# First norm's scale and shift terms as matrix-vector products between the dense products of the first three weight tiles

## Chip, cores and metric

One core of a Trainium2 chip runs the whole program. The metric is device time in microseconds (us); the kernel before takes 3083.03 us, the median of three runs (3082.98 to 3083.45).

## The reference, cut to what matters

Two layers work on 512 latent tokens and 256 context tokens of width 1024. Every sublayer starts with a modulated RMS norm, and the modulation comes from a conditioning vector (`c` for latent tokens, `c_ctx` for context tokens) through one large matrix with nine terms of 1024 per layer:

```
def modulate(h, g, shift, scale):
    return rmsnorm(h, g) * (1 + scale) + shift
def adaln_terms(s, w, b):
    return jnp.split(jax.nn.silu(s) @ w + b, N_MOD, -1)
def swiglu(x, w_up, w_down):
    gate, up = jnp.split(x @ w_up, 2, -1)
    return (jax.nn.silu(gate) * up) @ w_down
```

The first sublayer is a SwiGLU. Its up product can't be finished before term 0 (shift) and term 1 (scale) of layer 0 are known, each 1024 values for two vectors. These two terms are what the change is about.

## The kernel before, in words

Activations lie feature-major: `h` is 8 tiles (KD) of 128 features by 768 tokens. A list of items (`schedule`, L83) gives the order of work, and each engine's program walks that list. A dense product (`dense_step`, L1771) has one weight tile of up to 8 row blocks; for each block it issues six TensorE matmuls: high weights by high activations, high by low, low by high, each in two column pieces of 384 or 386. The split into high (`wh`) and low (`wl`) parts is made on the chip: ScalarE makes the high part (L988), GpSimd the low part (L883).

The norm is applied late: the activations that go in are `h * scale`, the factor 1/rms is applied to the product. The shift goes in as one more column for each of the two token kinds (`shift_high` L1037, `shift_low` L1321).

**The start item.** The first three weight tiles (FUSED = 3) are worked together, feature tile by feature tile: for k = 0..7 TensorE waits for the split activations of tile k (`late_lo`, `shift_lo`, L1826 and L1827) and then runs 18 matmuls, six for each of the three weight tiles. What stands before tile k:

- The scale term is a matrix-vector product on TensorE (`start_scale`, L1791): 8 products with a 128x128 weight block as stationary side and the 2 columns of `c_cols` as moving side. Each appears as two instructions in the trace. Blocks 0 and 1 run ahead of the dense work, block k+2 runs behind dense tile k. VectorE turns the result into the gain (`start_gains`, L1416).
- The shift term is made off TensorE from another layout of the weights (`ada_start`, 8 loads): VectorE multiplies and sums for the latent vector (`ada_chunk`, L1529), GpSimd multiplies for the context vector (`context_shift`, L892), ScalarE sums that (L1165), VectorE adds the bias (`start_shifts`, L1422). Both need the conditioning vectors spread over all partitions (`cb`), which TensorE makes with 16 products against the identity (L1817), copied by VectorE and ScalarE (L1559, L1163).
- ScalarE makes the high part of `h * scale` (`late_high`, L1054) and the square of `h` (L997), VectorE the low part (`late_low`, L1340), GpSimd sums the squares (`start_square`, L902).

After tile 7 the norm item (L1853) sums over the features, ScalarE takes the root (L1186), and from then on TensorE goes through dense products.

The loads are all asked by SyncE's queue, in this order: `scale_w` 0, `h` 0, three weight tiles, `ada_start` 0, and then `scale_w`, `h`, `ada_start` for k = 1..7 (L717 to L722), then constants.

Of the kernel before, what the change touches and what calls it, by code (L numbers as in the profile page):

```python
# [4 lines left out]

D = 1024
# [20 lines left out]
ADA_FIRST = KD  # L27
# [167 lines left out]
def build(nc, a, out, items):  # L195
# [8 lines left out]
    ada_order = ada_chunks(0, [0]) + [c for i in sorted(plan) for c in plan[i]]  # L204
    ada_no = {c: n for n, c in enumerate(ada_order)}
    term_no = {c[:2]: n for n, c in enumerate([c for c in ada_order[ADA_FIRST:] if c[2] == KD - 1])}
    on_dve = lambda n: n if n <= ADA_FIRST else 2 * n - ADA_FIRST
# [30 lines left out]
    with ExitStack() as ctx:  # L238
# [33 lines left out]
        def region(name):  # L272
# [9 lines left out]
        ada_start = [tb(f"ada_start{i}", [P, D]) for i in range(ADA_FIRST)]  # L282
# [45 lines left out]
        start_product, context_product = ada_w[2], ada_w[0:2]  # L328
# [27 lines left out]
        ident_loaded, const_loaded = sem("ident_loaded"), sem("const_loaded")  # L356
        c_rows_made, c_rows_copied, context_multiplied, context_summed = (
            sem("c_rows_made"), [sem(f"c_rows_copied{v}") for v in range(2)], sem("context_multiplied"), sem("context_summed"))
        c_cols_loaded, terms_loaded = sem("c_cols_loaded"), sem("terms_loaded")
        tile_loaded = [sem(f"tile_loaded{i}") for i in range(KD)]  # L360
# [4 lines left out]
        start_loaded = [sem(f"start_loaded{i}") for i in range(ADA_FIRST)]  # L365
# [46 lines left out]
        def released(x):  # L412
# [5 lines left out]
            if kind == "start":  # L418
                return [(start_gain, KD)]
# [71 lines left out]
        def c_rows(v):  # L491
            return psum[:, D * v:D * v + D]

# [13 lines left out]
        CONSTS = 16 * 5  # L507
# [190 lines left out]
        def _(sp):  # L698
# [13 lines left out]
            def load_start(k):  # L712

                sp.dma_start(scale_w[k][:, :], a["scale_w"][k]).then_inc(tile_loaded[k], 16)
                sp.dma_start(h[:, k, :], a["xT"][:, k, :]).then_inc(tile_loaded[k], 16)
# [7 lines left out]
            for dst, src in ((mean_w, "mean_w"), (ones_w, "ones_w"), (dn_w, "dn_w")):  # L723
# [45 lines left out]
            asked = [ADA_FIRST]  # L769
            last_even = max((slot_of[x] for x in proj_order), default=0)  # L770

            def load_ada(last):

                upto = ADA_FIRST + sum(len(plan[i]) for i in plan if i <= last)
                for n in range(asked[0], upto):
                    sp.wait_ge(ada_summed, on_dve(max(ADA_FIRST, n - ADA_BUFS + 1)))
# [3 lines left out]
            for x in items:  # L780
# [56 lines left out]
                if x[0] == "proj" and x[1] == 0:  # L837
                    k = proj_order.index(x) - 12
                    if k == 0:
                        sp.wait_ge(bias_made, 16 * 3 * ROWS * NA_HEADS)  # L840
                        sp.wait_ge(ada_summed, on_dve(ADA_FIRST + sum(len(c) for i, c in plan.items() if i < number[x])))
# [27 lines left out]
        def _(pool):  # L869
# [3 lines left out]
            done = [0]  # L873

            def split_up_to(n_slots):

                while done[0] < min(n_slots, len(slots)):
                    n = done[0]
                    _, k, w = slots[n]
                    if n:  # L880
                        pool.wait_ge(lo_split, n)
# [10 lines left out]
            def context_shift(k):  # L892

                pool.wait_ge(start_loaded[k], 16)
                if k == 0:
                    pool.wait_ge(c_rows_copied[1], 1)
                if k >= 2:
                    pool.wait_ge(context_summed, k - 1)
                nc.gpsimd.tensor_tensor(context_product[k % 2][:, :], ada_start[k][:, :], cb[:, 1, :], ALU.mult) \
                    .then_inc(context_multiplied, 1)  # L900

            def start_square(k):  # L902

                pool.wait_ge(squared, k + 1)
                if k == 0:
# [1266 lines left out]
```

## Time and profile before

| what | value |
|---|---|
| median of 3 runs | 3083.03 us |
| profiled execution, its own time | 3078.91 us |
| its span | 3077.1 us |
| mean granted TensorE clock | 0.991 of full |
| TensorE busy | 97% of the span |
| first dense matmul of the start item | 26.88 us |
| first dense matmul behind the first norm | 78.22 us |

The profiled execution is 4.1 us below the median of the runs; 1.8 us of its time lie outside the span. The last two lines bound the stage in which the change works: from there on the program before and after is the same.

### The profile page before, as it was taken

Reading aid. Unit: us, or ns where it says so; the run is one execution under the profiler, and the core shown is the slowest. Engines: PE = TensorE matmul, PEld = TensorE weight load, DVE = VectorE, ACT = ScalarE, POOL = GpSimd, SP = SyncE. Lnnn points to the kernel's source line nnn. Section 1 sums busy time; section 2 is a strip of 40 time slices with the busy share of each in tenths; the row PEclk is TensorE's granted clock in tenths of the full one; section 3 lists DMA queues with packets and bytes.
Section 4 is the critical chain, followed back from the end, with each engine's and each line's share of the span. In section 5 each row is a group of like instructions: output and inputs, shape, how many; then the busy total and the mean of one; then the engine's idle time right before and its main releaser. Section 6 shows DMA issues by size and latency. Waiting matters only on the chain.

```text
span 3077.1 us, 45850 instructions
## 1 busy us (share of the span) xinstructions
PE 2971.3 (97%) x19023; PEld 2783.6 (90%) x19023; DVE 1601.0 (52%) x2437; ACT 985.4 (32%) x1701; POOL 996.5 (32%) x516
## 2 busy tenths in 40 slices
PE   6999999999989988999999999999999999999998
PEld 6999999999888875899999999999999877798997
DVE  6556666884646666477677684212122358431223
ACT  4211212343454457322121233212122347532222
POOL 5333333333332202233333333222222222344442
PEclk8999999999999999999999999999999999999999
DMA  4434454223320022234344342121211210232222
GB/s 190 137 113 132 128 140 141 87 87 118 116 68 15 8 80 77 76 130 137 130 130 145 109 131 66 61 66 60 65 62 55 74 49 2 63 102 91 90 95 70
DMA packets 126236, 284.25 MB, mean 92 GB/s; under 512 B 40222, under 2 KB 57550, under 8 KB 126030
## 3 DMA queue, kind: packets, MB, share of 16 engines
q1 hardware_dynamic: 123150, 274.86, 28.0%
q10 hardware_dynamic: 2880, 6.47, 0.5%
q8 instruction: 151, 2.47, 0.3%
q14 instruction: 55, 0.45, 0.0%
HBM read 269.68 MB, written 15.10 MB: 93 GB/s over the span
## 4 chain that ended last, share of the span: by engine, by line
PE 88%; DVE 5%; ACT 4%; issue 2%; POOL 0%; DMA 0%; ACTq 0%; SPq 0%; DVEq 0%; POOLq 0%
PE psum L1777 78%; PE psum L1952 2%; PE psum L2052 1%; DVE o_acc L1604 1%; PE psum L2040 1%; ACT prob_o L1258 1%; DVE prob_o L1708 1%; PE psum L1937 1%; PE psum L2033 1%; PE psum L1993 1%; PE psum L1972 1%; PE psum L1959 1%; ACT cacc L1112 0%; PE psum L1982 0%; DVE probT_o L1720 0%
## 5 line engine op out<-in xcount | busy, mean ns | idle before, releaser
L883 POOL TENSOR_TENSOR wl<-raw,wh 128x1024 fp32r<-128x1024 f32 (+1 forms) x329 | 837.8, 2547 | 1649.3 <-ACT wh L988 1648.0
L1777 PE MATMUL psum<-uh,wh 128*128 128x256 f32 (+5 forms) x2704 | 660.5, 325 | 27.7 <-DVE ul L1325 17.6
L1777 PE MATMUL psum<-ul,wh 128*128 128x256 f32 (+5 forms) x2704 | 659.0, 325 | 0.0
L1777 PE MATMUL psum<-uh,wl 128*128 128x256 f32 (+5 forms) x2704 | 658.8, 325 | 0.0
L1777 PE MATMUL psum<-ah,wh 128*128 128x386 f32 (+4 forms) x2192 | 595.4, 344 | 4.7 <-POOL wl L883 3.5
L1777 PE MATMUL psum<-ah,wl 128*128 128x386 f32 (+4 forms) x2192 | 590.6, 342 | 0.0
L1777 PE MATMUL psum<-al,wh 128*128 128x386 f32 (+4 forms) x2192 | 588.3, 341 | 0.0
L1777 PEld LDWEIGHTS psum<-uh,wh 128*128 128x128 f32 (+1 forms) x2704 | 451.1, 189 | 51.7 <-issue 24.7
L1529 DVE SCALAR_TENSOR_TENSOR ada_product<-ada_w,cb 128x1024 f32<-128x1024 f32 x256 | 478.2, 1868 | 5.1
L1777 PEld LDWEIGHTS psum<-uh,wl 128*128 128x128 f32 (+1 forms) x2704 | 450.8, 189 | 19.7
L1777 PEld LDWEIGHTS psum<-ul,wh 128*128 128x128 f32 (+1 forms) x2704 | 450.2, 189 | 19.8
L988 ACT ACTIVATE wh<-raw 128x1024 fp32r<-128x1024 f32 (+1 forms) x329 | 336.5, 1025 | 391.5 <-PE psum L1777 380.7
L1777 PEld LDWEIGHTS psum<-ah,wh 128*128 128x128 f32 x2192 | 390.0, 189 | 27.3 <-issue 9.1
L1777 PEld LDWEIGHTS psum<-al,wh 128*128 128x128 f32 x2192 | 388.6, 189 | 18.4
L1777 PEld LDWEIGHTS psum<-ah,wl 128*128 128x128 f32 x2192 | 387.0, 189 | 18.2
L1739 DVE SCALAR_TENSOR_TENSOR h<-psum,mod,h 128x512 f32<-128x512 f32 x192 | 115.3, 635 | 363.9 <-PE psum L1777 363.9
L1365 DVE TENSOR_TENSOR af<-psum,rstd 128x770 f32<-128x770 f32 x66 | 63.3, 959 | 341.6 <-PE psum L1777 341.6
L1072 ACT ACTIVATE sg<-sg 128x512 f32<-128x512 f32 (+1 forms) x154 | 90.3, 628 | 460.0 <-DVE sg L1365 383.3
L1081 ACT ACTIVATE uh<-af 128x768 fp32r<-128x768 f32 x44 | 37.3, 847 | 313.1 <-DVE af L1377 313.1
L1365 DVE TENSOR_TENSOR sg<-psum,rstd 128x770 f32<-128x770 f32 x66 | 63.0, 955 | 115.9 <-PE psum L1777 115.8
L1377 DVE SCALAR_TENSOR_TENSOR af<-af,sg 128x512 f32<-128x512 f32 (+1 forms) x154 | 94.3, 648 | 4.2 <-ACT sg L1072 1.2
L1402 DVE SCALAR_TENSOR_TENSOR cacc<-sq,conv_w,cacc 128x254 f32<-128x254 f32 (+1 forms) x96 | 79.9, 873 | 1.3
(243 smaller groups left out, 2435.4 us busy)
## 6 DMA issues: line engine op xcount, KB each, us to landing
raw<-in_w SPq DMA_DIRECT2D x264, 512.0 KB, 3.6
ada_w<-in_ada_w SPq DMA_DIRECT2D x128, 512.0 KB, 3.8
raw<-in_w SPq DMA_DIRECT2D x64, 448.0 KB, 3.6
spill<-cacc ACTq DMA_DIRECT2D x16, 384.0 KB, 2.5
scale_w<-in_scale_w SPq DMA_DIRECT2D x8, 512.0 KB, 13.5
ada_start<-in_ada_w SPq DMA_DIRECT2D x8, 512.0 KB, 14.3
ada_w<-bias_final SPq DMA_DIRECT2D x16, 256.0 KB, 3.0
h<-in_xT SPq DMA_DIRECT2D x8, 384.0 KB, 13.7
```

The lines of the kernel that those rows point to most:

```text
L883: nc.gpsimd.tensor_tensor(wl[n % SPLIT_SLOTS][:, 0:k * w], raw[n % RAW_SLOTS][:, 0:k * w], wh[n % SPLIT_SLOTS][:, 0:k * w].bitcast(f32), A ...
L988: nc.scalar.activation(wh[n % SPLIT_SLOTS][:, 0:k * w], raw[n % RAW_SLOTS][:, 0:k * w], ACT.Copy).then_inc(hi_split, 1)
L1072: ins = nc.scalar.activation(t, t, ACT.Silu, bias=b)
L1081: ins = nc.scalar.activation(high[:, c, 0:T], af[g % 2][:, 1:1 + T], ACT.Copy)
L1258: nc.scalar.activation(p, p, ACT.Exp, bias=snb[:, u, a_:a_ + 1], scale=float(HD) ** -0.5, accum_out=sden[:, u, a_:a_ + 1]).then_inc(exp_do ...
L1365: nc.vector.tensor_tensor(t[:, :], bank[:, AT:AT + TU], rstd[rows_, :], ALU.mult).then_inc(scaled, 1)
L1377: ins = nc.vector.scalar_tensor_tensor(out=t, in0=t, scalar=b, in1=sg_part, op0=ALU.add, op1=ALU.mult)
L1402: ins = nc.vector.scalar_tensor_tensor(out=acc, in0=t[:, first + sh - lo:last + sh - lo], scalar=conv_w[:, c, j:j + 1], in1=acc, op0=ALU.m ...
L1529: nc.vector.scalar_tensor_tensor(out=product[:, :], in0=w[:, :], scalar=1.0, in1=cb[:, v, :], op0=ALU.mult, op1=ALU.mult, accum_out=mod[:, ...
L1739: ins = nc.vector.scalar_tensor_tensor(out=h[:, k, lo:hi], in0=banks_of(x)[:, lo:hi], scalar=mod[:, x[1], gate_term(x), k, v:v + 1], in1=h ...
L1777: ins = nc.tensor.matmul(pair[0:w, lo:hi], wt[n % SPLIT_SLOTS][:, k * w:(k + 1) * w], xt[:, k, cols], start=first, stop=last)
L1952: ins = nc.tensor.matmul(pair4(pair, 0)[:, hd, :], (dN[b] if k == 1 else dNI[d])[:, hd, :], dY[b][:, hd, :], start=True, stop=True)
```

## The change

Both terms are now made by `start_scale` and a new `start_shift_product` of the same form, from a second weight array `shift_w` in the layout of `scale_w`, loaded in the place of `ada_start`. Each writes one bank of its own. The products of tiles 0 and 1 run ahead of all dense work. Those of tile k+2 (16 products, 8 for each term) are laid into dense tile k: `dense_step` calls `beside` after each pair of matmuls, which issues the next two products, so that 8 of the 9 pairs of a tile are followed by two products (four instructions).

VectorE drops the eight products of the shift term and takes over the low split of the first three weight tiles (`split_low`) and the sum of the squares (`add_square`). GpSimd has no work in the start item any more. ScalarE drops its sums and the copy. The spread `cb`, still needed for later terms, is loaded by a broadcast DMA of 2048 values behind the start loads, and goes through a sigmoid on ScalarE and a product on VectorE. The identity is loaded on SyncE's queue behind the other constants.

```diff
-        start_product, context_product = ada_w[2], ada_w[0:2]
+        c_sigmoid = ada_w[0:2]
...
-                sp.dma_start(ada_start[k][:, :], a["ada_w"][ada_order[k]]).then_inc(start_loaded[k], 16)
+                sp.dma_start(shift_w[k][:, :], a["shift_w"][k]).then_inc(shift_loaded[k], 16)
...
+            sp.dma_start(cb[:, :, :].rearrange("p v k -> p (v k)"), a["cs"].to_broadcast([P, 2 * D])).then_inc(c_loaded, 16)
...
-            split_up_to(FUSED)
-            for k in range(KD):
-                context_shift(k)
-                if k:
-                    start_square(k - 1)
-            start_square(KD - 1)
...
             for k in range(KD):
-                act.wait_ge(tile_loaded[k], 32)
+                act.wait_ge(x_loaded[k], 16)
                 late_high(norm_items[0], k)
-                act.wait_ge(context_multiplied, k + 1)
-                nc.scalar.activation(context_product[k % 2][:, :], context_product[k % 2][:, :], ACT.Identity,
-                                     accum_out=mod[:, 0, 0, k, 1:2]).then_inc(context_summed, 1)
                 square(0, k)
+                if k == KD - 3:
+                    act.wait_ge(c_loaded, 16)
+                    for v in range(2):
+                        ins = nc.scalar.activation(c_sigmoid[v][:, :], cb[:, v, :], ACT.Sigmoid)
+                    ins.then_inc(sc_ready, 1)
...
+            split_low(0)
             for k in range(KD):
                 start_gains(k)
                 if k == 0:
+                    for n in range(1, FUSED):
+                        split_low(n)
-                ada_chunk(ada_order[k])
+                start_shifts(k)
+                if k:
+                    add_square(0, k - 1)
                 late_low(norm_items[0], k)
-                start_shifts(k)
...
+                    if beside:
+                        beside()
...
+            def start_shift_product(k, q):
+                if k and q == 0:
+                    pe.wait_ge(start_shift, k)
+                if q == 0:
+                    pe.wait_ge(shift_loaded[k], 16)
+                ins = nc.tensor.matmul(start_bank(1), shift_w[k][:, P * q:P * q + P], c_cols[:, q, :],
+                                       start=q == 0, stop=q == KD - 1)
...
-                    start_scale(0)
-                    pe.wait_ge(ident_loaded, 16)
...
-                    start_scale(1)
+                    start_terms(0, range(2 * KD))
+                    start_terms(1, range(2 * KD))
+                    pe.wait_ge(lo_split, FUSED)
                     for k in range(KD):
                         pe.wait_ge(late_lo, k + 1)
                         pe.wait_ge(shift_lo, k + 1)
+                        pieces = iter(range(2 * KD if k + 2 < KD else 0))
                         for y in fused:
-                            ins = dense_step(y, k, uh, ul)
+                            ins = dense_step(y, k, uh, ul, lambda: start_terms(k + 2, islice(pieces, 2)))
-                        if k + 2 < KD:
-                            start_scale(k + 2)
                     pe.wait_ge(start_gain, KD)
+                    pe.wait_ge(start_shift, KD)
```

## Rows read from the trace of the kernel before

**Rows 1.** The page: span, and busy time of each engine (share of span).

```profile
span 3077.1 us, 45850 instructions
...
PE 2971.3 (97%) x19023; PEld 2783.6 (90%) x19023; DVE 1601.0 (52%) x2437; ACT 985.4 (32%) x1701; POOL 996.5 (32%) x516
```

**Rows 2.** Chain of waits, 0 to 200 us: start, length, engine and line.

```profile
16.89 3.33 DVE ada_w L1529 x2
...
42.80 4.73 DVE ul L1340 x2
...
78.22 121.85 PE psum L1777 x689
```

**Rows 3.** TensorE's instructions in order of time: start, length, line, operands, count.

```profile
5.79 3.54 PE L1799 MATMUL psum<-c_cols,scale_w 128*128 128x2 f32 x16 [5.79 <-DMA h<-in_xT]
9.19 6.40 PE L1817 MATMUL psum<-ident,c_cols 128*128 128x128 f32 x32
...
26.88 0.98 PE L1777 MATMUL psum<-uh,wh 128*128 128x384 f32 x2 [9.61 <-DVE ul L1325]
27.66 0.85 PE L1777 MATMUL psum<-ul,wh 128*128 128x384 f32 x2
28.30 0.85 PE L1777 MATMUL psum<-uh,wl 128*128 128x384 f32 x2
...
31.95 0.52 PE L1777 MATMUL psum<-uh,wl 128*128 128x384 f32 x2
32.31 1.84 PE L1799 MATMUL psum<-c_cols,scale_w 128*128 128x2 f32 x16
34.01 0.60 PE L1777 MATMUL psum<-uh,wh 128*128 128x384 f32 x2
34.45 0.52 PE L1777 MATMUL psum<-ul,wh 128*128 128x384 f32 x2
34.80 0.52 PE L1777 MATMUL psum<-uh,wl 128*128 128x384 f32 x2
...
75.78 1.45 PE L1853 MATMUL psum<-sumsq,mean_w 128*128 128x512 f32 x4
78.22 0.62 PE L1777 MATMUL psum<-uh,wh 128*128 128x384 f32 x2 [0.99 <-ACT std L1186]
```

**Rows 4.** Stretches: length, busy PE PEld DVE ACT POOL, granted clock, DMA, GB/s.

```profile
5.80:14.50 8.70, 8.70 (x41) 8.70 (x42) 2.17 (x2) 4.29 (x5) 5.93 (x3) 1.00 1.03 407
14.60:18.00 3.40, 2.67 (x25) 2.59 (x23) 2.33 (x2) 1.02 (x1) 2.22 (x2) 1.00 1.02 406
18.00:26.80 8.80, 0.00 (x0) 0.00 (x0) 8.44 (x8) 2.18 (x5) 8.12 (x4) 0.50 1.03 406
26.90:31.60 4.70, 4.70 (x15) 4.70 (x16) 3.98 (x7) 3.08 (x7) 1.60 (x1) 0.50 1.03 409
...
45.40:52.10 6.70, 3.69 (x12) 3.72 (x13) 5.61 (x11) 3.38 (x9) 2.42 (x2) 0.50 0.00 0
...
62.40:78.20 15.80, 11.46 (x66) 10.23 (x64) 8.89 (x15) 9.16 (x18) 6.96 (x5) 1.00 0.00 0
```

**Rows 5.** VectorE's instructions in order of time.

```profile
42.73 4.80 DVE L1340 SCALAR_TENSOR_TENSOR ul<-h,mod,uh 128x512 fp32r<-128x512 f32 x2
...
48.37 1.22 DVE L1529 SCALAR_TENSOR_TENSOR ada_w<-ada_start,cb 128x1024 f32<-128x1024 f32 x1
...
49.70 1.15 DVE L1340 SCALAR_TENSOR_TENSOR ul<-h,mod,uh 128x512 fp32r<-128x512 f32 x2
```

**Rows 6.** ScalarE's instructions in order of time.

```profile
9.99 1.06 ACT L988 ACTIVATE wh<-raw 128x1024 fp32r<-128x1024 f32 x1 [0.22 <-DMA raw<-in_w]
```

**Rows 7.** SyncE's queue in order of time: first and last issue of `ada_start`.

```profile
3.15 0.60 SPq L722 DMA_DIRECT2D ada_start<-in_ada_w  x1
...
21.91 1.08 SPq L722 DMA_DIRECT2D ada_start<-in_ada_w  x1
```

**Rows 8.** The tile `ada_start`: time from issue to landing over its 8 loads.

```profile
DMA to landing us min/median/max: 8.1/14.3/15.5
```

More of the change, by code:

```diff
@@ L4 @@
 from contextlib import ExitStack
+from itertools import islice
 D = 1024
@@ L26 @@
 ADA_BUFS = 3
-ADA_FIRST = KD
 ADA_LAG = 4
@@ L281, in build @@
         scale_w = [tb(f"scale_w{i}", [P, D]) for i in range(KD)]
-        ada_start = [tb(f"ada_start{i}", [P, D]) for i in range(ADA_FIRST)]
+        shift_w = [tb(f"shift_w{i}", [P, D]) for i in range(KD)]
         guard.close()
@@ L364, in build @@
         raw_loaded = [sem(f"raw_loaded{i}") for i in range(RAW_SLOTS)]
-        start_loaded = [sem(f"start_loaded{i}") for i in range(ADA_FIRST)]
+        shift_loaded = [sem(f"shift_loaded{i}") for i in range(KD)]
         ada_loaded = [sem(f"ada_loaded{i}") for i in range(ADA_BUFS)]
@@ L418, in released @@
             if kind == "start":
-                return [(start_gain, KD)]
+                return [(start_gain, KD), (start_shift, KD)]
             if kind in RESIDUAL:
@@ L767, in load_nqk @@
                         .then_inc(nqk_loaded, 16)
-            asked = [ADA_FIRST]
+            asked = [0]
             last_even = max((slot_of[x] for x in proj_order), default=0)
             def load_ada(last):
-                upto = ADA_FIRST + sum(len(plan[i]) for i in plan if i <= last)
+                upto = sum(len(plan[i]) for i in plan if i <= last)
                 for n in range(asked[0], upto):
-                    sp.wait_ge(ada_summed, on_dve(max(ADA_FIRST, n - ADA_BUFS + 1)))
+                    if n >= ADA_BUFS:
+                        sp.wait_ge(ada_summed, on_dve(n - ADA_BUFS + 1))
+                    else:
+                        sp.wait_ge(sc_ready, 3)
                     sp.dma_start(ada_w[n % ADA_BUFS][:, :], a["ada_w"][ada_order[n]]).then_inc(ada_loaded[n % ADA_BUFS], 16)
@@ L840, in _ @@
                         sp.wait_ge(bias_made, 16 * 3 * ROWS * NA_HEADS)
-                        sp.wait_ge(ada_summed, on_dve(ADA_FIRST + sum(len(c) for i, c in plan.items() if i < number[x])))
+                        sp.wait_ge(ada_summed, on_dve(sum(len(c) for i, c in plan.items() if i < number[x])))
                         sp.dma_start(ada_w[2][:, 0:6 * P], a["m8"]).then_inc(m8_loaded, 16)
@@ L1056, in late_high @@
                 ins.then_inc(late_hi, 1)
+                if m == 0:
+                    act.wait_ge(start_shift, q + 1)
+                    shift_high(m, q, high).then_inc(shift_hi, 1)
             def conv_silu(c):
@@ L1519, in ada_chunk @@
                 n = ada_no[c]
-                if n < ADA_FIRST:
-                    dve.wait_ge(start_loaded[n], 16)
-                    w, product = ada_start[n], start_product
-                else:
-                    dve.wait_ge(ada_loaded[n % ADA_BUFS], 16 * ((n - ADA_FIRST - (n - ADA_FIRST) % ADA_BUFS) // ADA_BUFS + 1))
-                    w, product = ada_w[n % ADA_BUFS], ada_product
-                for v in range(2 if n >= ADA_FIRST else 1):
+                dve.wait_ge(ada_loaded[n % ADA_BUFS], 16 * (n // ADA_BUFS + 1))
+                w, product = ada_w[n % ADA_BUFS], ada_product
+                for v in range(2):
                     if on_dve(n) + v:
@@ L2142, in layouts @@
         "xT": feature_major(x),
+        "cs": np.concatenate([inputs["c"][0], inputs["c_ctx"]])[None],
         "c_cols": feature_major(np.stack([inputs["c"][0], inputs["c_ctx"]], 1)),
         "scale_w": np.stack([feature_major(inputs["ada_w"][0][:, D + P * j:D + P * j + P]).reshape(P, D) for j in range(KD)]),
+        "shift_w": np.stack([feature_major(inputs["ada_w"][0][:, P * j:P * j + P]).reshape(P, D) for j in range(KD)]),
         "ada_w": ada,
```

116 lines of the change are left out of this document (48 added, 68 removed).

## Prediction

> **What bounds the kernel now.** I read the page first: TensorE is busy for 97% of the 3077.1 us span [rows 1]. Then the chain of waits from the front: from 78.22 us it is one unbroken run of dense matmuls [rows 2], so whatever the start item saves or loses is saved or lost whole. The stage to be judged is what lies ahead of 78.22 us. In its chain stand VectorE pieces that are long for their size, 3.33 us for one product of 1024 and 4.73 us for two low splits [rows 2]; the same instructions take 1.22 and 1.15 us where GpSimd is quiet [rows 5]. So before, the start item is set by VectorE and GpSimd, and TensorE waits 9.61 us at once for its first dense matmul [rows 3]. Third, TensorE's own instructions and the granted clock by stretch, because the change moves work onto that engine.
>
> **Prices.** A block of 8 scale products (16 instructions) goes from 5.79 to 9.19 us: 3.40 us, 212 ns an instruction. The same block from 32.31 to 34.01 us takes 1.70 us, 106 ns an instruction [rows 3]. That is exactly half, so the first ran at 1.2 GHz and the second at 2.4. (The stretch view writes 1.00 for 5.8 to 14.5 us [rows 4]; the duration shows that it is the low level, the view has no record there yet.) A pair of dense matmuls goes in 0.64 us at 1.2 GHz (27.66 to 28.30) and in 0.35 us at 2.4 (34.45 to 34.80) [rows 3]. The first pair behind a block of scale products takes 0.44 us in place of 0.355 (34.01 to 34.45): coming back costs 0.085 us. Behind an idle engine at the low clock it was 0.78 in place of 0.64, 0.14 us [rows 3].
>
> **Part by part.** *Loads.* `shift_w` takes the place and size of `ada_start`; the first lands at 3.15 + 8.1 = 11.25 us, the last by 21.91 + 15.5 = 37.4 us [rows 7, 8]. Nothing is gained, and with the pace found below none but the first is waited for. The broadcast of `cb` is 1 MB behind that: at some 407 GB/s [rows 4] 2.6 us, there by about 42 us, long before ScalarE's tile 5. SyncE's queue gets one issue more; nobody waits for it.
>
> *Ahead of the dense work.* Removed: 16 products against the identity, 32 instructions from 9.19 us [rows 3]. Added: two blocks of shift products. Scale 0 ends by 9.2 us; shift 0 has to wait for its load, 11.25 to 14.65; scale 1 to 18.05; shift 1 to 21.45, each 3.40 us at the low clock. Beside it VectorE makes three low splits of 1024, at about 1.22 us each by its own product of that width [rows 5] (I take that; by the length of the row the bounds are 1.2 and 3.3 us, the long one only with GpSimd working, which it no longer does), after the last high split at 9.99 + 1.06 us [rows 6], and tile 0's low part by about 17.5 us. So the first dense matmul comes at 21.45 us against 26.88: 5.4 us gained.
>
> *Tiles 0 to 5, each with 16 products inside.* 9 dense pairs, 32 instructions, 8 returns. At 1.2 GHz: 9 x 0.64 + 32 x 0.2125 + 8 x 0.085 = 5.76 + 6.80 + 0.68 = 13.24 us. Bounds for the return, which the trace shows after a block of 16 but not after four instructions: 0 (12.56 us a tile) and 0.14 us (13.68); I take the row that follows scale products. At 2.4 GHz: 3.20 + 3.40 + 0.68 = 7.28 us (6.60 with no return cost). VectorE's work for a tile is now a low split of 1.15 us [rows 5], one sum of 768 and small pieces, about 3.5 us by the nearest rows; it hides under the tile before at either clock, and so does ScalarE's. Cost of the whole removal from VectorE and GpSimd: nothing left on the path, because TensorE is late next.
>
> *Which clock.* This decides. At 5.8 us TensorE becomes busy, and is busy without a gap up to 14.5 us, 8.70 of 8.70 us [rows 4]. If busy time alone raised the clock, then the 3.40 us of scale products would have counted like the rest; but the clock is still low while the identity products run: those have 32 instructions in 6.40 us, and only the stretch that they fill is followed by the high level from 14.6 us. Then scale block 1 runs, TensorE busy 2.67 of 3.40 us, and at 18.0 us the clock has gone back to 0.50 [rows 4], under 1 us after its last product. In contrast 62.4 to 78.2 us, with TensorE busy for 11.46 of 15.80 us, mostly dense, stayed at 1.00 [rows 4]. No stretch of scale products in this trace is followed by a rise, and one is followed by a fall. Every rise in this trace comes behind a stretch of unbroken full-width streaming: 4.70 us of dense matmuls to 31.6 us, and likewise at 52.1 us [rows 4]. The change has none of that before tile 6: it starts low, since nothing but 2-column products stands ahead of it, and tiles 0 to 5 never give the engine such a stretch. I take the low clock for all six.
>
> *Sum.* 21.45 + 6 x 13.24 = 100.9 us. Tiles 6 and 7 have no products inside, 18 pairs: 4.7 us low as in [rows 4] (7.3 pairs), the other 10.7 at 0.355 us, 8.5 us, to 109.4. Norm and root as before, 75.78 to 78.22 us [rows 3], 2.4 us: 111.8 us against 78.22, 33.6 us later. The rest is unchanged and TensorE-bound. Profiled execution: 3078.9 + 33.6 = 3112.5 us. Its own time is 4.1 us under the median of the runs; on the median's footing 3083.0 + 33.6 = 3116.6 us. With the bounds for the return, 29.6 to 36.3 us.
>
> **Rivals.** *A. The clock rises inside tile 0 and stays* (the other side: not slower). The place is the pairs of dense matmuls between the products; the point from which it decides is the first tile: whether dense pairs with four small instructions between them raise the clock as unbroken ones did. For it: TensorE is never idle there, and once high, 62.4 to 78.2 us shows that pauses don't lower it. Against: both readings at 5.8 and 18.0 us. After 4.7 us low (0.36 of a tile) come 5.64 x 7.28 = 41.1 us, to 67.3; tiles 6 and 7 take 6.4, norm 2.4: 76.1 us, 2.1 us earlier than before, 3081 us. Were the clock high from 14.6 us on (the earliest rise seen), the dense work would start by 17.5 us and the end be near 70 us: 3074 to 3075 us, the best case. So even with the clock, TensorE's own 6.8 us a tile eat most of what VectorE's stalls gave. [...]
>
> *B. The weight loads of the products hide under the dense matmuls.* Half of their cost would go: 5.76 + 3.40 + 0.68 = 9.84 us a tile, end at 21.45 + 59.0 + 8.5 + 2.4 = 91.4 us, 13.2 us later, 3096 us. For it: a dense matmul's load does hide, its pairs go at the streaming pace. Against: four instructions stand in a row, and three of their loads have nothing long above them. [...]
>
> *C. VectorE or ScalarE is late in place of TensorE*, by a load of `cb` or the squares. At 13.24 us a tile nothing of theirs reaches the path; with rival A the margin is 7.28 against about 3.5 us. It would add 2 to 5 us to A, 3083 to 3086 us.
>
> **How the numbers follow.** Forecast 0.62, A 0.24, B 0.08, C 0.04, something else 0.02. The predicted time is 3116 us; its own range is 3110 to 3122 (return cost, and up to 2 us for when the clock rises in tile 6). To leave out no more than two in ten, A has to be in: 3076 to 3121 us. A run of this kernel can be told from no change by about 0.2%, 6 us: faster means below 3076.9 us, the good end of A, 0.08; same is the rest of A and C, 0.20; slower the forecast and B, 0.72.
>
> **What would show it.** Granted clock 0.50 from about 15 us to about 105 us; the dense pairs of tiles 0 to 5 at 0.64 us with some 0.9 us between them; first dense matmul near 21.5 us, tile pitch near 13 us; no wait of TensorE on VectorE after tile 0; VectorE's low splits at 1.15 us throughout; the norm's matmul near 109 us. A clock of 1.00 in tile 1 and a pitch near 7 us would prove the forecast wrong and A right.

## Result and the profile after

| | before | after |
|---|---|---|
| median of 4 runs (us) | 3083.05 (3082.98 to 3083.45) | 3116.01 (3114.16 to 3116.34) |
| ratio, with its 95% interval | | 1.0105 [1.0093, 1.0117] |
| profiled execution, its own time and span (us) | 3078.91, 3077.1 | 3116.34, 3114.5 |
| first dense matmul of the start item (us) | 26.88 | 21.46 |
| first dense matmul behind the first norm (us) | 78.22 | 107.51 |

The change makes the kernel 33.0 us slower, 1.05%. By the two profiled executions 29.3 us lie ahead of the first dense matmul behind the norm (the "stage end" below), in the stage that the change rewrites. The other 3.7 us of the medians lie behind it, where both programs have the same instructions (18715 of TensorE each); only the weight buffers and waits of the later terms' first loads differ there. The ratios here and below go by fast executions; one of the 19 executions of before beside e1 to e4, of 3247.01 us, was a slow one.

The page of after: span, and busy time of each engine.

```profile
span 3114.5 us, 45986 instructions
PE 3023.2 (97%) x19119; PEld 2834.7 (91%) x19119; DVE 1577.1 (51%) x2433; ACT 978.1 (31%) x1686; POOL 956.7 (31%) x497
```

TensorE is busy 51.9 us longer than in [rows 1] with only 96 instructions more. 96 instructions at 106 or 212 ns are 10 or 20 us; the remainder is, in the main, work that was there before and now takes longer. TensorE's own rows of after, in order of time, say where:

```profile
5.33 3.58 PE L1781 MATMUL psum<-c_cols,scale_w 128*128 128x2 f32 x16 [5.33 <-DVE c_cols L1524]
11.19 3.58 PE L1792 MATMUL psum<-c_cols,shift_w 128*128 128x2 f32 x16 [2.28 <-DMA shift_w<-in_shift_w]
14.63 3.55 PE L1781 MATMUL psum<-c_cols,scale_w 128*128 128x2 f32 x16
18.04 3.55 PE L1792 MATMUL psum<-c_cols,shift_w 128*128 128x2 f32 x16
21.46 0.99 PE L1757 MATMUL psum<-uh,wh 128*128 128x384 f32 x2
22.24 0.85 PE L1781 MATMUL psum<-c_cols,scale_w 128*128 128x2 f32 x4
22.95 0.99 PE L1757 MATMUL psum<-ul,wh 128*128 128x384 f32 x2
23.74 0.85 PE L1781 MATMUL psum<-c_cols,scale_w 128*128 128x2 f32 x4
24.44 0.99 PE L1757 MATMUL psum<-uh,wl 128*128 128x384 f32 x2
...
97.16 0.85 PE L1757 MATMUL psum<-uh,wh 128*128 128x384 f32 x2
97.80 0.85 PE L1757 MATMUL psum<-ul,wh 128*128 128x384 f32 x2
...
100.84 0.51 PE L1757 MATMUL psum<-uh,wh 128*128 128x384 f32 x2
101.19 0.51 PE L1757 MATMUL psum<-ul,wh 128*128 128x384 f32 x2
...
105.07 1.45 PE L1846 MATMUL psum<-sumsq,mean_w 128*128 128x512 f32 x4
107.51 0.62 PE L1757 MATMUL psum<-uh,wh 128*128 128x384 f32 x2 [0.99 <-ACT std L1157]
```

Read the starts. Four blocks of small products stand ahead of all dense work, each 3.4 us from start to start: 16 instructions of 212 ns, the low level. Inside tile 0 a dense pair and two products (22.95 to 24.44 us) go in 1.49 us, and the two prices of the 1.2 GHz level in [rows 3] add up to the same, 0.64 + 4 x 0.2125. (The parts differ: 0.79 us for the pair, 0.70 for the four small instructions.) From 21.46 to 97.16 us that repeats: 75.70 us for six tiles, 12.6 us a tile. At 97.16 us the products end, and with them the gaps between dense pairs; at 100.84 us the pairs go at 0.35 us, the level of 2.4 GHz.

The stretches of after (columns as in [rows 4]: length, busy time of PE, PEld, DVE, ACT, POOL, granted clock, DMA share, GB/s):

```profile
5.30:21.40 16.10, 13.78 (x64) 13.70 (x65) 5.65 (x11) 6.33 (x10) 0.00 (x0) 1.00 1.03 409
21.50:97.10 75.60, 75.60 (x301) 75.60 (x302) 17.79 (x46) 16.58 (x37) 0.00 (x0) 1.00 0.27 105
97.20:100.40 3.20, 3.20 (x12) 3.20 (x11) 2.50 (x6) 0.63 (x1) 0.00 (x0) 1.00 0.00 0
```

TensorE is busy for 75.60 of 75.60 us, and VectorE and ScalarE for less than a quarter: the stage is now bound by TensorE alone. The clock column says 1.00 and is not to be believed here. It has no record before the first rise, at 100.57 us in this execution; the durations above say 1.2 GHz. The mean clock of the span (0.992, before 0.991) inherits that and hides the whole effect: someone who looks at it alone would rule the clock out.

The view of waits, 0 to 107 us (who waits for whom: us in total, times, longest):

```profile
DVE mod L1403 <- PE psum L1792: 39.9, 8, 5.7
...
DVE mod L1397 <- PE psum L1781: 25.5, 7, 4.3
```

The order of before is turned round: there TensorE waited for VectorE, now VectorE waits 65.4 us for TensorE's products, and no wait of TensorE on VectorE is left after tile 0. VectorE's pieces have the lengths forecast:

```profile
33.72 0.95 DVE L1290 TENSOR_TENSOR sumsq<-sumsq,sq 128x768 f32<-128x768 f32 x1
34.58 1.14 DVE L1311 SCALAR_TENSOR_TENSOR ul<-h,mod,uh 128x512 fp32r<-128x512 f32 x2
```

### The profile page after: what moved, and what is told of

The parts are those of the page before. It is cut to its first block, busy times and chain, and to the rows that moved or that the text cites. A ratio compares the mean times of both kernels' runs of the same rounds, so it can differ in the third digit from the quotient of the medians.

```text
span 3114.5 us, 45986 instructions
## 1 busy us (share of the span) xinstructions
PE 3023.2 (97%) x19119; PEld 2834.7 (91%) x19119; DVE 1577.1 (51%) x2433; ACT 978.1 (31%) x1686; POOL 956.7 (31%) x497
## 4 chain that ended last, share of the span: by engine, by line
PE 90%; DVE 4%; ACT 4%; issue 1%; DMA 0%; POOL 0%; SPq 0%; ACTq 0%; DVEq 0%; POOLq 0%
PE psum L1757 78%; PE psum L1945 2%; PE psum L2045 1%; DVE o_acc L1584 1%; PE psum L2033 1%; ACT prob_o L1229 1%; PE psum L2026 1%; PE psum L1930 1%; PE psum L1792 1%; DVE prob_o L1688 1%; PE psum L1986 1%; PE psum L1781 1%; PE psum L1965 1%; PE psum L1952 1%; ACT cacc L1088 0%
## 5 line engine op out<-in xcount | busy, mean ns | idle before, releaser
L1757 PE MATMUL psum<-ul,wh 128*128 128x256 f32 (+5 forms) x2704 | 667.3, 328 | 0.0
L1757 PE MATMUL psum<-uh,wl 128*128 128x256 f32 (+5 forms) x2704 | 667.1, 328 | 0.0
```

Of the source, the lines that this page charges most:

```text
L1757: ins = nc.tensor.matmul(pair[0:w, lo:hi], wt[n % SPLIT_SLOTS][:, k * w:(k + 1) * w], xt[:, k, cols], start=first, stop=last)
```

## The experiments

The theory after the result: the cost is the clock. TensorE is at 1.2 GHz from its first instruction, and dense pairs with four small instructions behind each don't bring it up, however busy the engine is. The rivals: the small products are dear as such (then the clock would not matter much), or the clock would fall again anyway as soon as such tiles run. A second question was why before takes 78 us, and a third where the 3.7 us behind the norm come from.

"Stage end" is the start of the first dense matmul behind the norm, "pitch" the time from the start of one dense tile to the start of the next. "Outside" is the difference of medians, against the runs of before beside the same kernels, less the difference of the stage ends (78.22 us before). The stage end is of one profiled execution, so it is good to a few us only.

| kernel | stage end | median (runs) | ratio [95%] | outside |
|---|---|---|---|---|
| after | 107.51 | 3116.01 (4) | 1.0105 [1.0093, 1.0117] | +3.7 |
| e1_block | 84.09 | 3088.68 (10) | 1.0024 [1.0014, 1.0035] | -0.3 |
| e2_warm | 76.88 | 3083.53 (10) | 1.0002 [0.9993, 1.0012] | +1.8 |
| e3_lead1 | 105.34 | 3113.50 (4) | 1.0101 [1.0083, 1.0119] | +3.3 |
| e4_early_lead1 | 111.25 | 3104.52 (4) | 1.0084 [1.0056, 1.0113] | see there |
| e5_half | 85.82 | 3093.51 (1) | none, one run | +2.0 |
| e6_quarter | 58.00 | 3062.73 (1) | none, one run | -0.9 |
| e7_before_noctx | 63.07 | 3068.14 (2) | 0.9951 [0.9933, 0.9969] | -0.6 |
| e8_held | 70.48 | 3078.94 (11) | 0.9983 [0.9974, 0.9992] | +2.8 |
| e9_delay | 108.03 | 3113.52 (4) | 1.0103 [1.0089, 1.0117] | +1.4 |
| e10_vector_both | 71.60 | 3080.28 (10) | 0.9992 [0.9982, 1.0001] | +4.6 |
| e11_vector_all | 64.45 | 3070.16 (5) | 0.9958 [0.9946, 0.9971] | +1.6 |
| e12_again | 107.08 | 3114.76 (4) | 1.0098 [1.0081, 1.0114] | +1.9 |

The medians of before beside them: 3083.06 (e1 to e4), 3083.88 (e5 to e8), 3082.32 (e9 to e11), 3083.95 (e12).

**e1_block: the same products, but behind a dense tile and not inside it.**

```diff
-                        pieces = iter(range(2 * KD if k + 2 < KD else 0))
...
-                            ins = dense_step(y, k, uh, ul, lambda: start_terms(k + 2, islice(pieces, 2)))
+                            ins = dense_step(y, k, uh, ul)
...
+                        if k + 2 < KD:
+                            start_terms(k + 2, range(2 * KD))
```

> The kernel after, with the 16 products of tile k+2 in one block behind dense tile k, not between its pairs. Theory (the low clock is the loss: it rises only behind unbroken dense matmuls): tile 0 is unbroken for 5.8 us and raises the clock before its end, near 27 us; a block of 32 small instructions is long enough to lose it again now and then, so the pitch of tiles 1 to 5 lies between 6.6 and 12.6 us, the first dense matmul behind the norm comes at 82 to 95 us, not at 107.5, and the kernel is 12 to 25 us faster than the changed one. Rival (the loss is the products' own work, wherever it lies): the same instructions, so 107.5 us within 1 us and no change of the median against the changed kernel.

Measured: stage end 84.09 us, in the expected 82 to 95, and by the medians 27.3 us of the 33.0 are gone though not one instruction is (12 to 25 were expected). Four of its stretches:

```profile
26.70:30.00 3.30, 3.30 (x31) 3.30 (x29) 0.28 (x1) 0.75 (x2) 0.00 (x0) 1.00 1.02 402
30.10:36.80 6.70, 6.70 (x24) 6.70 (x24) 2.28 (x6) 1.30 (x4) 0.00 (x0) 0.50 1.05 389
43.70:60.70 17.00, 17.00 (x128) 17.00 (x128) 5.27 (x15) 7.69 (x14) 0.00 (x0) 1.00 0.00 1
60.80:67.50 6.70, 6.70 (x27) 6.70 (x27) 3.94 (x9) 2.15 (x5) 0.00 (x0) 0.50 0.01 4
```

TensorE is busy for every microsecond of all four, and the clock goes up and down between them: up in unbroken dense work, down behind blocks of 32 small instructions (though not behind every one: the blocks that start at 45.15 and 51.91 us lie inside the 17 us at the high clock). So position decides, not the amount of work, and a full engine alone neither raises nor holds the clock.

**e2_warm: four products more.** Four unbroken products of 512 columns on constants between the last small product and tile 0; their result isn't used.

```diff
+            def warm(n, cols=512):
+                for _ in range(n):
+                    nc.tensor.matmul(psum[:, 0:cols], rstd[:, 0:P], rstd[:, P:P + cols], start=True, stop=True)
...
                     start_terms(1, range(2 * KD))
+                    pe.wait_ge(ones_set, 2)
+                    warm(4)
```

> The kernel after, with four additional unbroken products of 128x512 (constants, result unused) between the products of tile 1 and dense tile 0. Theory: they raise the clock, at a cost of 5 to 7 us ahead of tile 0 (dense start near 27.5 us), and once high it stays high through the tiles with products inside: pitch 6.6 us, first dense matmul behind the norm at 75 to 77 us, kernel 30 us faster than the changed one and 1 to 3 us faster than the one before the change. Rival (tiles with products between their pairs cannot hold the high clock either): it falls within the first such tile, pitch 12.6 us, 113 us, 5 to 6 us slower than the changed kernel.

Measured: stage end 76.88 us, in the expected 75 to 77; by the medians 32.5 of the 33.0 us are gone, by adding 5.7 us of work (21.53 to 27.22 us). The kernel was expected to be 1 to 3 us faster than before and is not: the medians differ by 0.5 us the other way, inside the interval. As in e8_held and e9_delay, GpSimd also fills a larger constant tile at the start, which isn't in the diff shown. The stretch and the rows:

```profile
26.70:74.40 47.70, 47.70 (x339) 47.16 (x338) 18.43 (x45) 17.73 (x36) 0.32 (x1) 1.00 0.32 122
```

```profile
21.53 6.25 PE L1775 MATMUL psum<-rstd 128*128 128x512 f32 x8
...
28.33 0.60 PE L1756 MATMUL psum<-ul,wh 128*128 128x384 f32 x2
28.77 0.50 PE L1785 MATMUL psum<-c_cols,scale_w 128*128 128x2 f32 x4
29.13 0.59 PE L1756 MATMUL psum<-uh,wl 128*128 128x384 f32 x2
```

Here a pair and its two products go in 0.80 us (28.33 to 29.13) in place of 1.49, and the pitch is 6.81 us in place of 12.6. The clock rose at 26.69 us, while the added products ran, and then held through six tiles of exactly the interleaved work of after. This is the proof for the clock, and it refutes that the interleaving by itself pulls a high clock down. It also prices the idea at its best: with the clock right, both terms on TensorE end the stage 1.3 us earlier than before and the median is the same.

**e3_lead1: a cheaper way to the same.** Tile 0 stays without products, so that it can raise the clock, and the terms of tile k+1 are laid into tile k (1 to 6). VectorE sums the squares last, so that the low split isn't behind them.

```diff
-                        pieces = iter(range(2 * KD if k + 2 < KD else 0))
+                        pieces = iter(range(2 * KD if 0 < k < KD - 1 else 0))
...
-                            ins = dense_step(y, k, uh, ul, lambda: start_terms(k + 2, islice(pieces, 2)))
+                            ins = dense_step(y, k, uh, ul, lambda: start_terms(k + 1, islice(pieces, 2)))
```

> The kernel after, with tile 0 left unbroken and the products of tile k+1 (not k+2) laid into tile k for k = 1 to 6; VectorE sums the squares last in each tile. No instruction of TensorE is added or taken away. Theory: tile 0's 5.8 us of unbroken matmuls raise the clock by about 27 us, and it holds: six tiles of 6.6 us and a wait of up to 1 us each for VectorE, behind the norm at 74 to 78 us, 29 to 33 us faster than the changed kernel. Rival (it cannot be held): back to 12.6 us a tile from tile 1 or 2 on, 105 to 112 us. Rival (a lead of one tile is too short for VectorE and ScalarE): waits of 3 us a tile, 90 us or more at the high clock.

Measured: stage end 105.34 us, nearly as slow as after, where 74 to 78 us were expected; the first rival's 105 to 112 us hold. Its stretches and one row:

```profile
26.90:37.10 10.20, 9.66 (x71) 9.37 (x71) 2.75 (x7) 2.15 (x5) 0.00 (x0) 1.00 1.04 394
37.20:101.90 64.70, 63.97 (x245) 61.57 (x245) 16.96 (x38) 15.19 (x30) 0.31 (x1) 0.50 0.07 26
```

```profile
34.58 0.59 PE L1757 MATMUL psum<-uh,wh 128*128 128x384 f32 x2 [0.54 <-DVE ul L1296]
```

Tile 0 did raise the clock, at 26.88 us, as expected; then it fell at 37.12 us and stayed low to 101.97. What this kernel has and e2_warm hasn't is a wait at each tile's start: with the terms only one tile ahead, TensorE idles 0.54 us for VectorE's last piece (34.58 us), and 0.54 us of 10.2 was all the idle time there was. My bet that the clock holds once it is up was too strong. This pause is the only difference from e2_warm that I see in the rows, and e4 shows the same, but no run varied the pause alone, so that it is the cause isn't shown. A pause by itself doesn't do it: e6_quarter waits 0.89 us once and e11_vector_all 1.61 us, both below, and the clock stays high.

**e4_early_lead1: more of both.** Seven products of 512 columns (four, one and two in a row) in TensorE's idle time ahead of the dense work, and the terms one tile ahead, from tile 0 on, with e3's order on VectorE.

```diff
+                    warm(4)
+                    start_terms(0, range(KD))
+                    warm(1)
+                    start_terms(0, range(KD, 2 * KD))
+                    warm(2)
...
+                            ins = dense_step(y, k, uh, ul, lambda: start_terms(k + 1, islice(pieces, 2)))
```

> The kernel after, with extra products of 128x512 on constants in the time in which TensorE waits for loads (four ahead of the first scale products, one and two more behind the first and second block), and the products of tile k+1 laid into tile k from k = 0 on, so that only those of tile 0 stand ahead of it. Theory: clock high by 8 us, dense start at 15 to 17 us, seven tiles of 6.6 us with up to 1 us of wait each, behind the norm at 67 to 74 us: 34 to 40 us faster than the changed kernel, 4 to 11 us faster than the one before. Rival (clock not held in the tiles): seven tiles of 12.6 us, 107 to 112 us.

Measured: stage end 111.25 us in the profiled execution, the worst of all, where 67 to 74 us were expected; it lies in the rival's 107 to 112. Stretches and row:

```profile
19.00:25.80 6.80, 6.26 (x46) 5.97 (x45) 2.27 (x7) 2.08 (x5) 0.00 (x0) 1.00 1.03 405
25.90:107.60 81.70, 80.82 (x312) 77.94 (x311) 19.72 (x45) 17.35 (x35) 0.00 (x0) 0.50 0.20 75
```

```profile
25.55 0.73 PE L1756 MATMUL psum<-uh,wh 128*128 128x384 f32 x2 [0.54 <-DVE ul L1295]
```

The clock was high from 5.3 to 12.2 us and from 19.0 to 25.8 us. The second time it fell beside the 0.54 us wait at 25.0 us, and then stayed low for 82 us. The profiled execution took 3118.8 us at a mean clock of 0.978, the three others 3101 to 3106 us at 0.982 to 0.986, so here the clock's course differs from one execution to the next, and its 111 us don't go with its median; that is why "outside" has no number.

**e5_half and e6_quarter: how much of the small work is too much?** The same places as in after, with 8 or 4 of the 16 products of a tile.

```diff
                 for n in pieces:
+                    if k >= 2 and n % KD not in (0, 3, 5, 7):
+                        continue
```

> The kernel after, with only 8 of the 16 products in each of tiles 0 to 5 (one, not two, behind each pair; the other half of the sums is left out). Theory: two effects, fewer products (32 to 16 instructions a tile, 3.4 us at the low clock) and perhaps a clock that rises. If it stays low: pitch 9.2 us, behind the norm at about 87 us. If it rises in tile 0: pitch 5.1 us, 62 to 66 us. I expect the rise, 0.6 to 0.4. Rival (the loss is the products' own work at one price each): pitch 9.2 us.

```diff
                 for n in pieces:
+                    if k >= 2 and n % KD not in (0, 7):
+                        continue
```

> The kernel after, with only 4 of the 16 products in each of tiles 0 to 5 (behind pairs 1, 4, 5 and 8; the rest of the sums is left out). Theory: the clock rises in tile 0 or 1 and holds; pitch 4.1 us, behind the norm at 55 to 60 us, unless the loads or VectorE set the pace (last shift weights land at about 37 us). Rival (the clock stays low behind any product laid between pairs): pitch 7.5 us, 77 us.

Measured: e5_half stayed at 1.2 GHz until 77.5 us (pitch of a tile 9.3 us, from 21.37 to 30.69) and ended its stage at 85.82 us; I had put 0.6 on a rise, wrongly, and its rival's number was the right one. Here too the clock column has no record before the rise and reads 1.00:

```profile
21.40:77.40 56.00, 56.00 (x208) 56.00 (x209) 18.67 (x47) 17.31 (x37) 0.00 (x0) 1.00 0.37 142
```

In e6_quarter the clock rose at 26.52 us and held, and the stage end, 58.00 us, is in the expected 55 to 60. TensorE's rows of e6_quarter across the rise:

```profile
24.54 0.99 PE L1757 MATMUL psum<-ul,wh 128*128 128x384 f32 x2
25.33 0.42 PE L1792 MATMUL psum<-c_cols,shift_w 128*128 128x2 f32 x2
25.61 0.99 PE L1757 MATMUL psum<-uh,wl 128*128 128x384 f32 x2
26.40 0.59 PE L1757 MATMUL psum<-uh,wh 128*128 128x384 f32 x2
26.82 0.52 PE L1757 MATMUL psum<-ul,wh 128*128 128x384 f32 x2
27.18 0.28 PE L1792 MATMUL psum<-c_cols,shift_w 128*128 128x2 f32 x2
```

For the clock the answer is a step, not a slope: 16 and 8 products a tile leave it low, 4 let it rise, and the stage end goes 107.51, 85.82, 58.00 us. Both kernels ran once. What isn't told apart is number and spacing: e5_half leaves one product behind each of eight pairs, while here three pairs follow one another between 25.61 and 27.18 us.

**e7_before_noctx: what bounds before?** Before, with GpSimd's and ScalarE's context half of the shift term left out.

```diff
-                context_shift(k)
...
-                act.wait_ge(context_multiplied, k + 1)
-                nc.scalar.activation(context_product[k % 2][:, :], context_product[k % 2][:, :], ACT.Identity,
-                                     accum_out=mod[:, 0, 0, k, 1:2]).then_inc(context_summed, 1)
+                nc.scalar.activation(mod[:, 0, 0, k, 1:2], ada_b[:, 0, 0, k:k + 1], ACT.Copy).then_inc(context_summed, 1)
```

> The kernel before, with the context half of the first shift term left out: GpSimd's eight products of 1024 and ScalarE's eight sums. Theory (before, the start item was set by VectorE stalled beside GpSimd, and by GpSimd's own chain): VectorE's 3.3 and 4.7 us pieces go back to 1.2 us, TensorE's waits shrink, the first dense matmul comes near 22 us and the one behind the norm at 58 to 66 us, 12 to 20 us earlier than the 78.2 of before. Rival (it was set by loads, or by the clock): within 3 us of 78.2.

Measured: stage end 63.07 us, 15.2 earlier, in the expected 58 to 66, and 15.7 us in the median. VectorE's rows:

```profile
43.50 1.15 DVE L1337 SCALAR_TENSOR_TENSOR ul<-h,mod,uh 128x512 fp32r<-128x512 f32 x2
44.56 1.80 DVE L1423 TENSOR_SCALAR mod<-mod,ada_b 128x2 f32<-128x2 f32 x1
```

The low splits that took 4.80 us in [rows 5] now take 1.15 at the same time of the run. VectorE did not have too much work before; it stood beside GpSimd's large products. Where GpSimd still sums squares, even a piece of two columns takes 1.80 us. Two things go with this run. GpSimd's own chain of products went too, and no run parts it from what it did to VectorE. And the clock is low for less of the dense work, from 20.3 to 23.7 us, where before TensorE was busy for 4.70 + 3.69 us at the low level [rows 4]; by half of the difference that is an estimated 2.5 us of the 15.2 at most.

**e8_held: hold the clock from the first microsecond.** After, with five unbroken products at 1.6 us, one more ahead of the shift products, and a 208-column product behind every two small ones ahead of tile 0.

```diff
+                    warm(5)
+                    for k in range(2):
+                        for n in range(0, 2 * KD, 2):
+                            if (k, n) == (0, KD):
+                                warm(1)
+                            start_terms(k, range(n, n + 2))
+                            warm(1, 208)
```

> The kernel after, with extra products on constants: five unbroken ones of 128x512 from 1.6 us, one more before the first shift products, and one of 128x208 behind every two of the 32 products that stand ahead of tile 0. Theory (the clock is raised by unbroken wide matmuls and held by wide ones laid between the narrow ones): clock high by 8.5 us and never low before the norm, dense start at 20 to 22 us, six tiles of 6.7 us, behind the norm at 68 to 72 us; 6 to 10 us faster than the kernel before, 0.2 to 0.3%, and 38 to 42 us faster than the changed one. Rival (it falls once, in the blocks ahead, and tile 0 starts low): six tiles at 12.6 us, 105 us or more.

Measured: stage end 70.48 us, in the expected 68 to 72.

```profile
4.90:21.00 16.10, 16.10 (x104) 14.07 (x103) 5.84 (x13) 6.56 (x11) 0.00 (x0) 1.00 1.03 408
21.10:68.00 46.90, 46.90 (x338) 46.90 (x337) 20.17 (x51) 18.75 (x39) 0.32 (x1) 1.00 0.45 173
```

High from 4.85 us to the norm. The stage is 7.7 us shorter than before, but the median only 4.9 us, below the 6 to 10 us expected: 2.8 us come back outside.

**e9_delay: does it matter behind the norm when the stage ends?** Before, with 34 unbroken products of 512 columns ahead of norm 0 and, but for GpSimd's larger constant tile, nothing else changed.

```diff
                     pe.wait_ge(start_gain, KD)
+                    pe.wait_ge(ones_set, 2)
+                    warm(34)
```

> The kernel before, with 34 unbroken products of 128x512 on constants (result unused) between dense tile 7 and the first norm: at 0.853 us each 29.0 us, so that everything behind the norm runs as late as in the changed kernel, and nothing else differs. It asks where the part of the loss comes from that does not lie in the start item (the changed kernel is 33.0 us slower by the medians, 29.3 us of it ahead of the norm). Theory (the pauses of TensorE behind the norm are the same, and whether the clock falls in them is a matter of when they come): 3083.1 + 29.0 + 2 to 5 us = 3114 to 3117 us. Rival (something in the changed kernel other than time makes its later part longer, such as the order of loads or of GpSimd's work): 3112 us within 1 us.

Measured: the stage ends at 108.03 us, 29.8 later, as in after; the median is 31.2 us above that of before beside it (30.5 above 3083.05). A mere delay costs 1.4 us outside, of after's 3.7, between the two numbers expected; neither theory is shown.

**e10_vector_both and e11_vector_all: the other way round.** If e7 is right, what is to be taken from GpSimd should go to VectorE, and TensorE be left alone. In e10 VectorE makes both halves of the shift term by the old route; in e11 it sums the squares as well, and GpSimd has only the low split of the three weight tiles left in the stage (10.2 us busy of 64.5).

```diff
-    on_dve = lambda n: n if n <= ADA_FIRST else 2 * n - ADA_FIRST
+    on_dve = lambda n: 2 * n
...
-                context_shift(k)
...
-                for v in range(2 if n >= ADA_FIRST else 1):
+                for v in range(2):
```

> The kernel before, with the context half of the first shift term moved from GpSimd and ScalarE to VectorE (a second product with sum of 1024 for each tile, 1.3 us). Theory (before, GpSimd's work beside VectorE's was the loss, not VectorE's own work): TensorE's own work is 4.9 us a tile at the high clock, VectorE's chain 6 to 6.5 us with the squares still summed by GpSimd; behind the norm at 68 to 73 us, 5 to 10 us faster than before. Rival (VectorE's own work was the bound): 8 x 1.3 = 10 us more, 88 us.

```diff
-                if k:
-                    start_square(k - 1)
-            start_square(KD - 1)
...
                 start_shifts(k)
+                if k:
+                    add_square(0, k - 1)
```

> As e10_vector_both, and the squares summed by VectorE too (0.95 us a tile), so that GpSimd has no work in the start item but the low split of three weight tiles. Theory: no VectorE instruction is stretched any more, chain 5.5 to 6 us a tile, behind the norm at 64 to 69 us; 10 to 14 us faster than before, 0.3 to 0.45%, the best of the kernels so far. Rival (VectorE is full): 1 us a tile slower than e10_vector_both.

Measured: stage ends 71.60 and 64.45 us, both in the expected stretches. The median of e10 is only 2.0 us below before, with a ratio interval that holds 1, where 5 to 10 us were expected; that of e11 is 12.2 us below, in the expected 10 to 14. VectorE's rows, e10 and then e11:

```profile
44.47 2.70 DVE L1336 SCALAR_TENSOR_TENSOR ul<-h,mod,uh 128x512 fp32r<-128x512 f32 x2
```

```profile
43.74 1.22 DVE L1524 SCALAR_TENSOR_TENSOR ada_w<-ada_start,cb 128x1024 f32<-128x1024 f32 x1
45.00 1.23 DVE L1524 SCALAR_TENSOR_TENSOR ada_w<-ada_start,cb 128x1024 f32<-128x1024 f32 x1
46.15 1.14 DVE L1334 SCALAR_TENSOR_TENSOR ul<-h,mod,uh 128x512 fp32r<-128x512 f32 x2
47.34 0.95 DVE L1313 TENSOR_TENSOR sumsq<-sumsq,sq 128x768 f32<-128x768 f32 x1
48.71 0.28 DVE L1413 TENSOR_SCALAR mod<-psum,scale_one,norm_g 128x2 f32<-128x2 f32 x1 [0.28 <-PE psum L1796]
```

VectorE has more to do in e11 than in before and is busy for 41.7 us of the stage in place of 50.2: the pieces shown have their short lengths, and from one start to the next (43.55 and 48.71 us) a tile takes 5.16 us with 0.28 us of waiting for TensorE in it. The two engines are in step, and TensorE's stretch from the rise of the clock to the norm shows 1.83 us of waits with the clock still high:

```profile
25.20:62.00 36.80, 34.97 (x231) 34.51 (x230) 30.75 (x71) 16.27 (x36) 0.35 (x1) 1.00 0.39 147
```

e11 is the best version found that leaves nothing out: 3070.16 us, 12.2 us (0.42%) below the runs of before beside it, and 46 us below after.

**e12_again: after, unchanged, once more.**

> The changed kernel once more, nothing edited, to see how much of its loss behind the norm belongs to one execution. Theory (clock falls in TensorE's pauses differ from execution to execution): the start item repeats within 0.3 us (first dense matmul behind the norm at 107.2 to 107.8), the part behind it differs by 1 to 6 us from the 3007.0 us of the first profile, and the low stretches there have other lengths. Rival (they belong to the kernel): the same low stretches at the same places, 3007 us within 0.5 us.

Measured: the stage ends at 107.08 us, 0.1 us short of the expected 107.2 to 107.8, since the clock rose 2.2 us into tile 6 and not 3.4. Behind it lie 3113.1 - 107.08 = 3006.0 us, against 3114.5 - 107.51 = 3007.0 in the first profile: 1.0 us less, the lowest that the theory gave and outside the rival's 0.5. One of its four executions took 3108.73 us. So the time behind the norm mostly repeats, but the outside of after is 1.9 us here and 3.7 in the first set, and its median 3114.76 us, not 3116.01.

## Why the prediction was right, and what in it was not

Forecast 3116 us, measured 3116.01. The agreement is closer than the steps deserve: two errors of some 4 us cancel, and that is luck. The mechanism, low clock through the six tiles, was right.

- **What bounds the kernel before** (VectorE beside GpSimd, TensorE waiting): right. e7 and e11 show it from both sides, with stage ends 15.2 and 13.8 us earlier; at most some 2.5 us of either is the clock's. How much was GpSimd's own chain and how much what it did to VectorE isn't told apart.
- **Ahead of the dense work**: 21.45 us forecast, 21.46 measured. Every term stood: the shift load (11.25 forecast, 11.19), four blocks at the low clock.
- **Which clock**: right, and it is the step that carries the sign. Low through tiles 0 to 5, shown by the durations and by e2_warm, where raising the clock takes away 32.5 of the 33.0 us. The reason given, that only unbroken full-width work is followed by a rise, was right in its direction and too strict: in e6_quarter the clock rose with four products among a tile's nine pairs. The Trainium skill, "TensorE: Matmul & The Clock Gate", section "Why this matters for your kernels", gives keeping TensorE busy without a break as the way to the highest matmul throughput. After was busy for 75.60 of 75.60 us at the low clock, so being busy was not enough here, and the measurement decides.
- **Price of a tile**: 13.24 us forecast, 12.6 measured. The term that was mis-sized is the return from small products to a dense pair together with the small instructions beside it. The pair behind them takes 0.79 us (22.95 to 23.74), 0.15 above the 0.64, where 0.085 was taken from a row at the high clock; but the four small instructions take 0.70 us (23.74 to 24.44), not 4 x 0.2125 = 0.85. The two cancel, and a pair and two products cost 1.49 us, as with the lower bound of the return, 0. At the high clock it is the same within 0.02 us: 0.44 + 0.36 = 0.80 us in e2_warm (28.33, 28.77, 29.13), against 0.355 + 0.425. So a return read behind a block of 16 is no price for four. Six tiles were put too long by 6 x 0.62 = 3.7 us.
- **Tiles 6 and 7**: 8.5 us forecast, 7.9 measured (97.16 to 105.07); the clock rose 3.4 us into them, not 4.7. Norm: 2.4, measured 2.44.
- So the stage was forecast to end at 111.8 us and ended at 107.5: 29.3 us later than before, just under the 29.6 that the sum gave with no return.
- **"The rest is unchanged"**: wrong by +3.7 us, or +1.9 by e12_again. This is the error that hides the other. The instructions there are the same, yet stretches at the low clock fall differently. The same loop of the attention part, after and then before:

```profile
2551.30:2558.20 6.90, 5.46 (x32) 4.33 (x32) 3.86 (x13) 3.78 (x9) 1.66 (x4) 0.51 0.01 2
```

```profile
2518.90:2525.80 6.90, 6.12 (x65) 4.65 (x64) 4.46 (x15) 5.34 (x13) 1.65 (x4) 1.00 0.01 2
```

65 instructions against 32 in the same time. By the clock records of the two traces the clock is low for 53.2 us behind the norm in after and for 36.9 us in before. At half speed 16.3 us more cost 8.1 us at most (an estimate), and 8.1 us is what the two profiles differ by behind the norm. The table's last column shows that nearly every kernel with a moved stage end has such a remainder, -0.9 to +4.6 us, also e9_delay, which has none of the change. The profiled execution of before had the least of it: 2998.9 us behind the norm, against 3001.8 to 3007.0 in all others. That fits the 37.4 us between the two profiles, where the medians differ by 33.0. The low time orders the kernels only roughly (e1_block 33.6 us low and 3001.8 behind the norm, e2_warm 39.8 and 3004.9, e9_delay 55.4 and 3005.4), and why the clock is low for longer in one kernel than in another stays open.

- **Rivals.** A (the clock rises by itself and stays) didn't happen. Its 76.1 us lie near the 76.88 of e2_warm by luck: e2_warm starts its dense work 5.8 us later, has no low stretch in tile 0, and its tiles take 6.81 us, not 7.28, the same mis-sized term. What spoke for A, that pauses don't lower the clock once it is high, is in doubt for interleaved tiles: in e3 and e4 it fell beside one. B (loads hidden, 91.4 us) would have made a pair and two products 0.64 + 0.425 + 0.085 = 1.15 us; they took 1.49. C never came up: VectorE was busy for 17.79 us in six tiles, 3.0 us of each 12.6.

## What to carry to other kernels

Before moving small work onto TensorE, price it at both clock levels and look for what in the new order would raise the clock: thin products between dense pairs can keep the engine full and at half speed together. If such work must go there, give the clock unbroken wide products first and leave no wait between the interleaved tiles behind them (the two kernels that had one lost the high clock), and read the level from durations of one known instruction, not from the clock column alone. And where an engine seems overloaded, look first whether its instructions are long only beside another's; moving GpSimd's products and sums onto VectorE won 12.2 us here, and the best kernel that relieved VectorE instead, e8_held, 4.9.

## What the runs showed of the hardware that was not expected

- 16 or 8 thin products among a tile's nine dense pairs kept TensorE at 1.2 GHz for 76 and 56 us in which it was busy throughout; 4 let it rise at 26.52 us, as early as unbroken work did (26.69 in e2_warm).
- Rising and holding ask for different things: six tiles of interleaved work held a high clock for 40.9 us in e2_warm (27.22 to 68.08) and did not raise it in 75.7 us in after. Beside waits of 0.54 us it was lost, and then not regained for 65 and 82 us (e3, e4); in e11, with its products in blocks, it outlasted a wait of 1.61 us.
- The same program can take different courses of the clock: e4 3101 to 3119 us at mean clocks of 0.986 to 0.978, e1 3082 to 3098 us at 0.991 to 0.986, where the executions of before, but for the one of 3247 us, lie between 3078 and 3085.
- VectorE's product of 1024 and its low split take 1.22 and 1.15 us where GpSimd is quiet; beside GpSimd's products they took up to 3.33 and 4.80 us, and the low split 2.70 us beside its sums of squares (e10).
